# The third and fourth gate chunk of a decoder layer as one pair of 512 columns

## The reference, cut to what matters

```python
x   = layer_norm(alpha * x + mix, ln1_g[i], ln1_b[i])
ple = sigmoid(x @ w_ple_gate[i]) * (p[i] @ w_ple_proj[i])
x   = layer_norm(alpha * x + conv_ffn(x, w_up[i], conv_w[i], conv_b[i], w_down[i]) + ple, ln2_g[i], ln2_b[i])
```

## Time and profile before

| | |
|---|---|
| median of 3 runs | 1502.68 us (1502.22 to 1502.71) |
| profiled execution | 1502.79 us |
| its span | 1501.0 us |
| PE busy | 1485.1 us (99%), 8706 matmuls |
| DVE busy | 997.5 us (66%) |
| ACT busy | 787.3 us (52%) |
| granted TensorE clock, mean | 0.999 |

### The profile page before, as it was taken

The page is one execution under the profiler, slowest core; times in us unless marked ns, Lnnn a source line. Parts: engine busy times, 40 slices in busy tenths (PEclk is TensorE's granted clock), DMA queues, the critical chain, the costliest instruction groups (busy, mean ns, idle before and its releaser), DMA issues.

```text
span 1501.0 us, 20912 instructions
## 1 busy us (share of the span) xinstructions
PE 1485.1 (99%) x8706; PEld 1316.0 (88%) x8706; DVE 997.5 (66%) x1113; ACT 787.3 (52%) x829; POOL 45.0 (3%) x24
## 2 busy tenths in 40 slices
PE   8999999999999999999999999999999999999998
PEld 7898898988988988888888988989889888888886
DVE  5575665756655688777866656666566556887777
ACT  5464464554654456556544645536446444666562
POOL 0000000000000010000010000000000000100000
PEclk9999999999999999999999999999999999999999
DMA  9544545455456465656555554455445565655561
GB/s 294 195 145 164 169 141 196 141 168 169 168 169 207 172 215 177 200 193 223 168 169 169 169 168 145 165 171 166 158 151 172 173 216 169 212 199 191 170 238 40
DMA packets 231470, 265.83 MB, mean 177 GB/s; under 512 B 4192, under 2 KB 221792, under 8 KB 230752
## 3 DMA queue, kind: packets, MB, share of 16 engines
q1 hardware_dynamic: 231248, 264.57, 53.0%
q10 hardware_dynamic: 144, 0.13, 0.0%
HBM read 263.64 MB, written 1.05 MB: 176 GB/s over the span
## 4 chain that ended last, share of the span: by engine, by line
PE 94%; DVE 4%; ACT 1%; issue 1%; DMA 0%; DVEq 0%; SPq 0%; ACTq 0%
PE bank L1249 35%; PE bank L1253 18%; PE bank L1223 9%; PE bank L1225 8%; PE bank L1224 8%; PE acc L1223 3%; PE acc L1224 3%; PE acc L1225 3%; PE acc L1391 1%; PE acc L1366 1%; DVE w_lo L722 1%; PE acc L1346 1%; PE acc L1389 1%; PE acc L1362 1%; ACT w_hi L391 1%
## 5 line engine op out<-in xcount | busy, mean ns | idle before, releaser
L722 DVE TENSOR_TENSOR w_lo<-raw,w_hi 128x2048 fp32r<-128x2048 f32 x240 | 549.6, 2290 | 272.0 <-ACT w_hi L391 271.6
L391 ACT ACTIVATE w_hi<-raw 128x2048 fp32r<-128x2048 f32 x243 | 463.7, 1909 | 142.5 <-PE bank L1225 81.3
L1249 PE MATMUL bank<-xT_both,w_hi 128*128 128x512 f32 x1952 | 489.4, 393 | 0.0
L1249 PEld LDWEIGHTS bank<-xT_both,w_hi 128*128 128x128 f32 x1952 | 352.2, 189 | 64.1 <-issue 0.4
L1253 PEld LDWEIGHTS bank<-xT_both,w_lo 128*128 128x128 f32 x1952 | 266.3, 190 | 19.0
L1253 PE MATMUL bank<-xT_both,w_lo 128*128 128x256 f32 x1952 | 272.2, 282 | 0.0
L1223 PE MATMUL bank<-w_hi,xT_both 128*128 128x256 f32 (+1 forms) x528 | 176.9, 335 | 4.8 <-DVE w_lo L722 1.8
L1225 PE MATMUL bank<-w_hi,xT_both 128*128 128x256 f32 (+1 forms) x528 | 175.6, 333 | 0.0
L1224 PE MATMUL bank<-w_lo,xT_both 128*128 128x256 f32 (+1 forms) x528 | 175.6, 333 | 0.0
L490 ACT ACTIVATE scratch<-bank 128x512 f32<-128x512 f32 x64 | 38.3, 598 | 222.4 <-PE bank L1253 222.4
L1223 PEld LDWEIGHTS bank<-w_hi,xT_both 128*128 128x128 f32 x528 | 101.0, 191 | 16.5 <-issue 6.4
(11 more groups left out here) (169 smaller groups left out, 1612.8 us busy)
## 6 DMA issues: line engine op xcount, KB each, us to landing
raw<-w_in SPq DMA_DIRECT2D x135, 1024.0 KB, 5.0
raw<-w_up SPq DMA_DIRECT2D x44, 1024.0 KB, 5.1
raw<-w_down SPq DMA_DIRECT2D x20, 1024.0 KB, 5.0
raw<-w_ret_proj SPq DMA_DIRECT2D x16, 1024.0 KB, 5.2
raw<-w_attn_proj SPq DMA_DIRECT2D x8, 1024.0 KB, 5.1
raw<-w_out SPq DMA_DIRECT2D x8, 1024.0 KB, 4.9
raw<-w_ple_gate SPq DMA_DIRECT2D x8, 1024.0 KB, 5.1
scratch<-ln_rows SPq DMA_DIRECT2D x4, 1024.0 KB, 7.8
```

Of the source, the lines that this page charges most:

```text
L391: nc.scalar.activation(w_hi[:, s, :], raw[:, s, :], ACT.Copy).then_inc(hi_ready, 1)
L722: nc.vector.tensor_tensor(w_lo[:, s, :], raw[:, s, :], w_hi[:, s, :].bitcast(F32), ALU.subtract).then_inc(lo_ready, 1)
L1249: mm(pair[p][:, m, :], hi[:, o:o + P], src[:, k0 + k, :, :].rearrange("p a t -> p (a t)"), start=first and k == 0, stop=False)
```

## The change

G3 and G4 are computed together by `two_chunks`: for token tile 0 both chunks' 512 columns into `bank[2]`, then for token tile 1 into `bank[3]`. So each of these banks holds one token tile and the columns 512 to 1023. PE waits for the `w_lo` of G4 before the first matmul of the pair. ACT's third sigmoid waits for `tile_done`, its fourth for `chunk_done` of the pair. DVE's third and fourth product and residual cover one token tile and 512 columns instead of two tiles and 256 columns. The `to_hi` and `to_lo` of U2, which needs the slot of G3, move behind the fourth sigmoid and the fourth residual. `tiles_before` counts one event more for layer 1.

```diff
         def tiles_before(l, j):
-            return 7 + 2 * j if l else max(2 * j - 1, 0)
+            return 8 + 2 * j if l else max(2 * j - 1, 0)
...
                     if j:
                         act.wait_ge(ple_ready, l * NJ + j)
-                    copy_out(L0, C_PLE + 2 + j, j, ple_sig, func=ACT.Sigmoid)
+                    if j < 2:
+                        copy_out(L0, C_PLE + 2 + j, j, ple_sig, func=ACT.Sigmoid)
+                    if j == 2:
+                        act.wait_ge(tile_done, tiles_before(l, NJ) + 1)
+                    if j == 3:
+                        act.wait_ge(chunk_done, L0 + C_PLE + 5 + 1 + RING)
+                    if j >= 2:
+                        nc.scalar.activation(ple_sig, bank[j][:, :], ACT.Sigmoid).then_inc(bank_read[j], 1)
                     if j == 2:
                         act.wait_ge(last_loaded, 16 * (l + 1))
                         nc.scalar.activation(last_hi, last_raw, ACT.Copy).then_inc(last_hi_ready, 1)
-                        to_hi(l, L0 + C_MLP, R0 + 16 * C_MLP // RING, 1)
+                to_hi(l, L0 + C_MLP, R0 + 16 * C_MLP // RING, 1)
...
-                    v = ple[:, :, j * CH:(j + 1) * CH]
-                    nc.vector.tensor_tensor(v, v, ple_sig.rearrange("p (t n) -> p t n", t=TT), ALU.mult)\
-                      .then_inc(ple_ready, 1)
+                    part = (slice(None), slice(None), slice(j * CH, (j + 1) * CH))
+                    by = ple_sig.rearrange("p (t n) -> p t n", t=TT)
+                    if j >= 2:
+                        part, by = (slice(None), j - 2, slice(2 * CH, 4 * CH)), ple_sig
+                    v, x = ple[part], X[part]
+                    nc.vector.tensor_tensor(v, v, by, ALU.mult).then_inc(ple_ready, 1)
                     dve.wait_ge(ple_ready, l * NJ + j + 1)
-                    x = X[:, :, j * CH:(j + 1) * CH]
                     nc.vector.scalar_tensor_tensor(out=x, in0=x, scalar=ALPHA, in1=v,
                                                    op0=ALU.mult, op1=ALU.add).then_inc(residual_ready, 1)
                     if j == 2:
                         dve.wait_ge(last_hi_ready, l + 1)
                         nc.vector.tensor_tensor(last_lo, last_raw, last_hi.bitcast(F32), ALU.subtract)\
                           .then_inc(last_lo_ready, 1)
-                        to_lo(l, L0 + C_MLP, 1)
+                to_lo(l, L0 + C_MLP, 1)
...
-                for j in range(2, NJ):
-                    pe.wait_ge(bank_read[j], l * USES[j] + (U_PLE[j] + 2))
-                    by_token(l, L0, C_PLE + 2 + j, j)
+                weights_ready(L0, C_PLE + 5)
+                for t in range(TT):
+                    pe.wait_ge(bank_read[2 + t], l * USES[2 + t] + (U_PLE[2 + t] + 2))
+                    two_chunks(l, C_PLE + 4, 2 + t, t)
```

## The result

| | before | changed |
|---|---|---|
| median | 1502.80 us (22 runs, 1502.22 to 1504.91) | 1505.32 us (22 runs, 1504.78 to 1507.08) |
| profiled execution, its span | 1502.79, 1501.0 us | 1505.09, 1503.3 us |
| PE, matmuls | 1485.1 us, 8706 | 1484.4 us, 8610 |

The ratio is 1.0016, 95% interval 1.0010 to 1.0022.

A forecast was written before the change was run, and what follows sets the result against it. PE, busy 99% of the span, was taken as the bound. Per layer, 1.76 us of wait less 0.52 saved gives +1.24, +2.48 for both, hence 1505.2 us (+0.17%), with an 8-in-10 range of 1504.2 to 1506.3 us.

The forecast's parts named there:

- The saving: PE, G3 and G4: 48 matmuls of 512 columns replace 96 of 256, saving 0.52 us per layer.
- my 11.00: PE, the pair: 11.00 us for 48 wide matmuls, taken from the same function on value chunks, slow first step included.
- the 11.52: PE, kernel before: 11.52 us for G3's and G4's 96 narrow matmuls, from 557.63 to 569.15.
- The wait: PE, head of the pair: idle for G4's low part from 557.63 to 559.39, 1.76 us per layer.
- The sum: PE, start of U1: 570.39 instead of 569.15, +1.24 us per layer, +2.48 us for both, 1505.2 us in total.
- What moved behind the pair at no cost: ACT, DVE and DMAs after the pair: later sigmoids, U2 and U3 conversions, sums and transfers add nothing.
- the narrowest place: PE, start of U2: weights available at 575.51, wanted at 575.98, a margin of 0.47 us.
- (a): Rival at U2: a second PE wait behind sigmoid 4, 0.53 us more per layer, 1506.3 us; chance 10%.
- (b): Rival at the pair: wide matmuls save nothing, leaving 3.52 us of waiting, 1506.2 us; chance 3%.
- (c): Rival at the pair's head: G4's low part comes before 557.63, only the saving is left, 1501.6 us; chance 4%.
- (d): Rival at a later stage: held by a transfer or DVE, it swallows the delay, 1502.7 us; chance 3%.
- (e): Rival at the pair: idling lowers PE's clock, 0.48 us per matmul, 12.2 us more per layer, 1529.6 us; chance 2%.

The follow-up runs named there:

- wait_only: Kernel before plus one PE wait for G4's low part ahead of G3, matmuls still 256 columns wide: 1506.90 us, ratio 1.0027.
- late_u2: Changed kernel with three extra sigmoids into unread scratch ahead of sigmoid 4, putting off U2's conversion by 1.5 us: 1509.19 us.
- u2_first: Changed kernel with ACT converting U2 before sigmoid 4, as the kernel before did, both still after the pair: 1507.33 us.
- split_pair: Changed kernel, PE doing three k-blocks of G2's tile 0, then G1's tile 1, G2's rest, the pair: 1501.81 us, ratio 0.9992 to the kernel before.
- long_wait: Changed kernel with PE waiting at the head of the pair for U1's low part instead of G4's: 1516.10 us.

## Why the prediction was right, point by point

**The saving.** Foretold 0.52 us per layer, with 0.228 us per wide matmul. The pair took 11.01 us against 11.00. But my 11.00 held a slow first step and the 11.52 did not. Nor was it a step after a wait, as I wrote: the pair of the earlier trace rows follows eight matmuls of 128 columns without idle time:

```profile
112.39 1.04 PE L1346 MATMUL acc<-const,scratch 128*128 128x128 f32 x8
```

That its first step (0.32 us) is as long as the one after the wait (0.33 us, 559.34 to 559.67) was luck; no row ahead of the prediction showed it. Like for like the width is worth 0.60: 11.61 - 11.01 after a wait (wait_only against the change), 11.52 - 10.90 = 0.62 without one. By an estimate from the isolated spacing of N / 2.4 + 2.5 ns in the Trainium skill (TensorE: Matmul & The Clock Gate, "Back-to-back issue gap") this would have been 0.12; the runs decide for the rows.

**The wait.** Foretold a start at 559.39, measured 559.34: PE began 0.06 us after DVE's end, where I had taken 0.14 from one row. It came free 0.03 us later and so stood for 1.68 us instead of 1.76. By wait_only the wait costs 1.76 all the same, 1.67 of standing and 0.09 of the slow first step (foretold 1.84 there).

**The sum.** U1 at 570.39, measured 570.35; +1.24 per layer, measured +1.17; +2.48 in all, measured 2.3 by the span and 2.5 by the medians. 1505.2 us against 1505.32.

**What moved behind the pair at no cost.** Sigmoid 3 at 565.2 (565.16), sigmoid 4 at 570.65 (570.61), U2's conversion at 571.15 (571.10), its subtraction from 573.08 (573.04), a margin of 0.47 (0.42 by late_u2), the sum of U1's bank at 577.6 (577.45). PE did not wait for U2. The claim that this is the narrowest place was tested by late_u2, and u2_first broke it unasked.

**Rivals.** (a), a second wait at U2, did not come, but it is a real mechanism: late_u2 shows 1.06 us of it per layer once the chain is 1.5 us longer. (b) and (c) fell with split_pair and wait_only: the width does save, the wait does bite. (d) fell with the span: the delay was not swallowed. Its "waits are 1.8 us in sum" was misread, since 1.8 us are the waits for L722 alone; the list for the kernel before comes to 8.6 us. 4.9 us of that lie in the first 12 us of the program, so the argument survives. (e) did not come at 1.7 us, where the granted clock stayed full, and did at 5.2 us. My price for it (0.48 us for every matmul of the pair) was too high by far: nine steps were slow, most of 0.426 us, and they cost 1.88 us and not 12.2.

**What was off.** I expected PE's wait for L722 to grow from 1.8 to about 5.3 us; the list says 4.8. The list counts idle time from the modelled end of the last matmul (557.54 + 0.28), not from the moment at which the next could have been issued (557.66), so it shows 1.52 us for a stand of 1.68.

## What to carry to other kernels

Merging two operations also merges their waits: the first now starts when the later of both inputs is there. Before two products are made one, compare what the width saves with how long the second input would hold up the first; here 0.6 us against 1.8. If the input is late because of a buffer, see whether the last reader of that buffer can be moved forward: splitting G2's first tile did it for 0.05 us and turned a loss of 2.5 us into a gain of about 1, which the length of the stage shows and the whole-run times only suggest.

## What the runs showed of the hardware, unexpected

**The clock after a stand.** A wait of 1.7 us in running matmuls left the granted clock at 1.00, one of 5.2 us took it to 0.50. That a stand can do this is what the Trainium skill says (TensorE: Matmul & The Clock Gate, "Why this matters for your kernels"), and the trace of long_wait agrees. The slow matmuls cost 1.88 us in layer 0 and 1.76 in layer 1, about half of the 3.5 us of extra waiting that caused it.

**The start of the program differs by one or two microseconds.** Runs of one kernel spread over up to some 2.8 us. In the profile of split_pair the start went another way than in those of the kernel before and of the changed one. Granted clock is the number behind the busy count:

```profile
4.00:8.00 4.00, 1.96 (x13) 1.00 0.76 241
8.00:12.00 4.00, 2.28 (x9) 0.50 1.05 384
12.00:16.00 4.00, 4.00 (x25) 0.65 1.10 349
```

The changed kernel has 1.00 in these three stretches. With the low clock the first narrow matmuls came every 0.21 us instead of 0.12, and the gates' stage began at 549.99 instead of 548.95. So this one profiled execution took 1502.65 us, while the median of that kernel is 1501.81. In the trace of long_wait the clock reads 1.00 there, and yet its first narrow matmuls are as slow:

```profile
11.87 0.41 PE L1233 MATMUL bank<-w_lo,xT_both 128*128 128x256 f32 x1
12.08 0.41 PE L1234 MATMUL bank<-w_hi,xT_both 128*128 128x256 f32 x1
...
12.00:16.00 4.00, 4.00 (x21) 1.00 1.10 357
```

Its stage began 2.04 us late. At the start the spacing of the matmuls tells more than the clock that is listed. For effects of one microsecond the length of the stage told more than whole runs.
